# Two-term MLP up products: one 512-column matmul for two of 256, and a split evacuation

## The reference

```python
def _sq_relu_mlp(h, w_up, w_down):
    u = jax.nn.relu(h @ w_up)
    return (u * u) @ w_down
```

## Time and profile before

| | us |
|---|---|
| median of 3 runs | 1383.15 (1383.14 to 1383.69) |
| span of the profiled execution | 1382.5 |
| TensorE busy | 1346.9 (97%) |
| VectorE busy | 864.3 (63%) |
| ScalarE busy | 673.8 (49%) |
| mean granted TensorE clock | 0.991 |

### The profile page before, as it was taken

One profiled execution on the slowest core, in us unless ns is written; L12 is line 12 of the kernel. 1 busy time (PEld: TensorE's weight loads), 2 busy tenths in 40 slices (PEclk: granted clock), 3 DMA queues, 4 the chain that ended last, 5 costly groups with the idle time before them and its releaser, 6 DMA issues.

```text
span 1382.5 us, 26707 instructions
## 1 busy us (share of the span) xinstructions
PE 1346.9 (97%) x11635; PEld 1195.1 (86%) x11635; DVE 864.3 (63%) x1388; ACT 673.8 (49%) x1202; POOL 87.7 (6%) x104
## 2 busy tenths in 40 slices
PE   8999999999999999999999999999999998999997
PEld 6888998988867889998799999799987896799996
DVE  6786655573395655556685666856467556856565
ACT  6775544552384545442651224445443468545452
POOL 3000400000060000000000430000000000000000
PEclk9999999999999999999999999999999999999999
DMA  9345555453302555554233000655545451555550
GB/s 350 124 182 198 183 183 183 183 198 123 147 38 68 193 189 188 196 191 151 105 140 123 4 5 34 240 200 184 183 183 183 153 183 62 179 193 190 199 184 31
DMA packets 17635, 215.18 MB, mean 156 GB/s; under 512 B 1976, under 2 KB 2144, under 8 KB 4848
## 3 DMA queue, kind: packets, MB, share of 16 engines
q1 hardware_dynamic: 15888, 205.54, 40.3%
q0 software_dynamic: 1632, 7.94, 1.6%
HBM read 212.41 MB, written 1.06 MB: 154 GB/s over the span
## 4 chain that ended last, share of the span: by engine, by line
PE 84%; DVE 9%; ACT 4%; DMA 1%; issue 1%; SPq 0%; DVEq 0%; ACTq 0%
PE psum L665 24%; PE psum L471 11%; PE psum L472 11%; PE psum L473 11%; PE psum L1008 3%; DVE w_low L1862 3%; PE psum L1089 2%; PE psum L569 1%; PE psum L1141 1%; ACT w_high L1342 1%; PE psum L540 1%; PE psum L565 1%; PE psum L541 1%; PE psum L542 1%; DMA ring<-weights 1%; PE psum L561 1%
## 5 line engine op out<-in xcount | busy, mean ns | idle before, releaser
L1862 DVE TENSOR_TENSOR w_low<-ring,w_high 128x1024 fp32r<-128x1024 f32 x368 | 437.0, 1222 | 231.7 <-ACT w_high L1342 231.7
L1342 ACT ACTIVATE w_high<-ring 128x1024 fp32r<-128x1024 f32 x368 | 368.6, 1047 | 175.9 <-PE psum L665 155.4
L471 PE MATMUL psum<-act_split,w_high 128*128 128x256 f32 x1312 | 381.7, 291 | 3.7 <-DVE w_low L1862 3.6
L472 PE MATMUL psum<-act_split,w_high 128*128 128x256 f32 x1312 | 372.5, 284 | 0.0
L473 PE MATMUL psum<-act_split,w_low 128*128 128x256 f32 x1312 | 372.3, 284 | 0.0
L665 PE MATMUL psum<-w_high,up_split 128*128 128x512 f32 x1024 | 287.6, 391 | 0.8 <-DVE up_split L2010 0.8
L471 PEld LDWEIGHTS psum<-act_split,w_high 128*128 128x128 f32 x1312 | 252.6, 193 | 11.6 <-DVE w_low L1862 4.7
L472 PEld LDWEIGHTS psum<-act_split,w_high 128*128 128x128 f32 x1312 | 253.0, 193 | 2.6 <-issue 1.4
L473 PEld LDWEIGHTS psum<-act_split,w_low 128*128 128x128 f32 x1312 | 252.9, 193 | 0.0
L665 PEld LDWEIGHTS psum<-w_high,up_split 128*128 128x128 f32 x1024 | 190.4, 188 | 40.5 <-issue 2.7
L665 PE MATMUL psum<-w_low,up_split 128*128 128x512 f32 x512 | 163.1, 390 | 0.0
(11 more groups left out here) (338 smaller groups left out, 1661.3 us busy)
## 6 DMA issues: line engine op xcount, KB each, us to landing
ring<-weights SPq DMA_DIRECT2D x95, 2048.0 KB, 7.8
work<-rows POOLq DMA_DIRECT2D x4, 1024.0 KB, 5.0
ring<-weights SPq DMA_DIRECT2D x4, 512.0 KB, 8.5
work<-rows POOLq DMA_DIRECT2D x4, 512.0 KB, 5.6
x<-x_in SPq DMA_DIRECT2D x2, 512.0 KB, 4.4
work<-t_bias POOLq DMA_DIRECT2D x1, 1024.0 KB, 8.9
out<-x SPq DMA_DIRECT2D x4, 256.0 KB, 2.0
con<-consts SPq DMA_DIRECT2D x1, 687.0 KB, 21.6
```

What stands on the lines that cost most here:

```text
L471: mm(out, w_hi, x_hi, start=start, stop=False)
L472: mm(out, w_hi, x_lo, start=False, stop=False)
L1342: A(high[:, HIGH_SLOT[name], f], ring[:, n % RING, f], ACT.Copy).then_inc(weights_high, 1)
L1862: V.tensor_tensor(low[:, n % RING, f], ring[:, n % RING, f], high[:, HIGH_SLOT[name], f].bitcast(f32), ALU.subtract).then_inc(weights_spli ...
```

## The change

In blocks 1 to 7 the high weights meet high and low activations in one matmul of 512 columns, which leaves high x high in the first and high x low in the second half of the bank; low x high is added to the first half by a matmul of 256 columns. The two halves have to be added, and the ReLU comes after that. ScalarE copies the second half into `up_sum` (the former `up_relu`). VectorE waits for it (`up_cross`), adds the first half from PSUM, which also gives the bank back, waits with `settle()` for its own result, and computes max(sum, 0) * sum in one instruction.

```diff
--- before.py
+++ after.py
@@ -240,7 +240,7 @@
         scales = work[:, 16, :].rearrange("p (r d) -> p r d", r=2)
 
         up_split = over("up_split", 6, [P, 4, 2, T])
-        up_relu = work[:, 7, 0:1024].rearrange("p (m t) -> p m t", m=4)
+        up_sum = work[:, 7, 0:1024].rearrange("p (m t) -> p m t", m=4)
         up_sq = work[:, 7, 1024:2048].rearrange("p (m t) -> p m t", m=4)
         up_relu_tokens = work[:, 7, 0:1024].rearrange("p (h f) -> p h f", h=2)
         up_sq_tokens = work[:, 7, 1024:2048].rearrange("p (h f) -> p h f", h=2)
@@ -652,8 +652,10 @@
                             if m == 0 and k % 2 == 0:
                                 quarter_in(name, k // 2)
                             at = k * 512 + m * P
-                            last = product(bank(q, T), w_hi[:, at:at + P], w_lo[:, at:at + P],
-                                           act_split[:, k, 0, :], act_split[:, k, 1, :], k == 0, k == NC - 1)
+                            mm(bank(q), w_hi[:, at:at + P], act_split[:, k, :, :].rearrange("p s t -> p (s t)"),
+                               start=(k == 0), stop=False, skip_group_check=True)
+                            last = mm(bank(q, T), w_lo[:, at:at + P], act_split[:, k, 0, :], start=False,
+                                      stop=(k == NC - 1), skip_group_check=True)
                         last.then_inc(bank_filled, 1)
 
                     name = f"down{layer}_{b}"
@@ -1435,7 +1437,7 @@
                         split(f"down{layer}_{b}", [m])
                         q = TURN[("up", layer, b)] + m
                         filled(q)
-                        taken(A(up_relu[:, m, :], bank(q, T), ACT.Relu), q)
+                        A(up_sum[:, m, :], bank(q)[:, T:2 * T], ACT.Copy).then_inc(sig("up_cross"), 1)
                         act.wait_ge(sig("up_squared"), 4 * (FBLOCKS - 1) * layer + 4 * (b - 1) + m + 1)
                         A(up_split[:, m, 0, :], up_sq[:, m, :], ACT.Copy).then_inc(sig("up_high"), 1)
                     if b < FBLOCKS - 1:
@@ -2003,9 +2005,11 @@
                         split(f"down{layer}_{b}", [m])
                         q = TURN[("up", layer, b)] + m
                         at = 4 * (FBLOCKS - 1) * layer + 4 * (b - 1) + m + 1
-                        read_out(dve, q)
-                        V.tensor_tensor(up_sq[:, m, :], up_relu[:, m, :], up_relu[:, m, :],
-                                        ALU.mult).then_inc(sig("up_squared"), 1)
+                        dve.wait_ge(sig("up_cross"), at)
+                        taken(V.tensor_tensor(up_sum[:, m, :], bank(q, T), up_sum[:, m, :], ALU.add), q)
+                        settle()
+                        V.scalar_tensor_tensor(up_sq[:, m, :], up_sum[:, m, :], 0.0, up_sum[:, m, :],
+                                               ALU.max, ALU.mult).then_inc(sig("up_squared"), 1)
                         dve.wait_ge(sig("up_high"), at)
                         V.tensor_tensor(up_split[:, m, 1, :], up_sq[:, m, :], up_split[:, m, 0, :].bitcast(f32),
                                         ALU.subtract).then_inc(sig("up_split"), 1)
```

## The result

| | before | after |
|---|---|---|
| median of 4 runs, us | 1383.42 | 1390.12 (1388.39 to 1390.71) |
| ratio | | 1.0047 [1.0034, 1.0061] |
| span of the profiled execution, us | 1382.5 | 1388.9 |
| mean granted TensorE clock | 0.991 | 0.989 |

The kernel became 0.5% slower; the forecast was 1383.9, no measurable difference, and the range ended at 1387.3.

The account below looks back on a forecast made before the run. TensorE, busy 97% of the span, was taken as the bound, with block 7 waiting on evacuation. 1382.5 - 9.6 + 7.0 + 2 x 1.7 gave a span of 1383.3 us, a median of 1383.9; range 1380.3 to 1387.3.

Parts of the forecast that it names:

- The period of the blocks: Blocks 1 to 6 of four layers: TensorE is the bound, 0.40 us less a block, 9.6 us in all.
- The cover for the longer evacuation: Blocks 1 to 6: m-tile 3 ready 1.7 us later stays hidden, with 1.4 us of cover left.
- The price of the pair: Up product, blocks 1 to 7: 512 plus 256 columns take 347.2 ns where three 256-column matmuls took 359.7.
- The bound of 0 to 12.5: Up product: limits in ns on what a pair saves against three 256-column matmuls; 12.5 was taken.
- The evacuation: Block 7: 0.46 us more per m-tile, ready 1.74 us later, 7.0 us in four layers; TensorE stop about 2.2 us.
- The clock: After block 7's four stops: the granted TensorE clock falls, 1.7 us each, two falls likeliest.
- one to three: Number of block 7's four stops followed by a clock fall; 1382.2 to 1385.6 us, chance 0.60.
- The sum: Profiled span: 1382.5 - 9.6 + 7.0, plus 2 x 1.7, is 1383.3 us; median of runs 1383.9.
- The pair saves nothing: Rival: blocks 1 to 6 gain 0 and block 7 loses 7.4 us, giving 1390.5 us; chance 0.06.
- The rival with a saving of 2.5 ns: Up product: a pair saves only the skill page's fixed part, 1.9 us in 24 blocks, giving 1388.5 us.
- The clock falls after every one: Rival: a clock fall after all four block 7 stops, 4 x 1.7 us, giving 1387.3 us; chance 0.12.
- The clock never falls: Rival: no clock fall after block 7's stops, only -9.6 + 7.0 left, giving 1380.5 us; chance 0.17.

Follow-up runs that it names:

- e1: The kernel before with streams of single and mixed matmul widths appended after TensorE's last product; a 512/256 pair took 346.7 ns, total time not compared.
- e9: The kernel before with appended streams of 512/256 pairs entered from different widths; 353 ns a pair behind 512 columns, 346.8 behind 384; total time not compared.
- e4: The kernel before with the new pairs of 512 and 256 columns but the old evacuation; 1382.06 us against 1383.74, ratio 0.9979.
- e6: The kernel before with appended streams of pairs using the up product's own weights, activations and banks, and variants; 352.8 ns a pair as it is.
- e3: The changed kernel with the old widths, three 256-column matmuls per k-chunk, keeping the new evacuation; 1394.19 us, ratio 1.0077 against the kernel before.
- e5: The changed kernel with each m-tile's eight 512-column matmuls ahead of its eight 256-column ones; 1384.29 us, ratio 1.0011 against the kernel before.
- e7: The changed kernel with eight matmuls of zeros where TensorE stops in block 7 of each layer; 1386.82 us, ratio 1.0028 against the kernel before.

## Why the prediction was wrong

- **The period of the blocks.** Right that blocks 1 to 6 are bound by PE and that a saving there reaches the end: six periods brought six times 0.19 us. The cover for the longer evacuation held; no wait of the up product for low weights appeared.
- **The price of the pair: the step that failed.** "I take 12.5, because the down stretch changes its weights at every matmul as the new one does, and both slots are read from unbroken streams." The pair took 353 ns, not 347.2, and the down product took 0.03 us more a block: 24 x 0.19 = 4.5 us in place of 9.6. The bound of 0 to 12.5 held it; the upper end was taken. The reason was not good enough: adding the slots of two unbroken streams assumes that a stream of both runs at the sum. e1 shows that it can (346.7), e9 that behind 512 columns, which is what stands ahead in this kernel, it runs at 353; e4 shows the 353 without the new evacuation, e6 without anything beside.
- **The evacuation.** Right in its size: copy 0.39, the dependent operation 0.45 us behind the add, multiply 425 ns (424 taken), a turn of 3.46 us, a stop of 2.2. The last layer, whose stop left the clock alone, shows it bare: +1.78 us where 1.74 was worked out. e3 shows that the stop comes with the evacuation: 8.2 us of it in the four layers without the pairs, 8.7 with them.
- **The clock.** The price of a fall was right (1.64 against 1.7), the number not: three falls, two forecast, inside "one to three". Over the changed kernel, e3 and e5 the clock fell behind 8 of 12 stops of 2.0 to 2.3 us, not always in the same layers. So I read the count as a chance for each stop of that length, which one execution of each kernel can't prove; at two in three the likeliest count is three, 1.6 us more than I added. The prediction's own rows, three falls behind four stops, said so already, and it counted two.
- **The sum.** -4.5 + 7.0 + 4.9 = +7.4, against +6.4 in the span and +6.7 in the medians. Of the miss of 6.2 us, 5.1 is the pair and 1.5 the clock, less 0.4 that the stretches around gave back, where the clock of one execution differs from that of another.
- **The rivals.** "The pair saves nothing" came out nearest in time (1390.5) by luck. It saves half, and the 1390.5 left out the two falls that the forecast counted; with them it would have been 1393.9, and e3, where the pair is absent and the clock fell three times, took 1394.19. The rival with a saving of 2.5 ns left them out too, 1388.5 where 1391.9 would have stood. The Trainium skill (TensorE: Matmul & The Clock Gate, Back-to-back issue gap) has those 2.5 ns as the fixed part of an isolated matmul, and by them, as an estimate, a pair would save 2.5 ns. The traces show 6.6 ns in the kernel and 13.0 in e1 (359.7 - 346.7), so the measurements decide against it. "The clock falls after every one" was one fall away. "The clock never falls" failed: eight falls stand behind stops of 2.0 to 2.3 us. The Trainium skill (TensorE: Matmul & The Clock Gate, Why this matters for your kernels) warns only of gaps longer than these, and the measurements decide against that too.
- **The range** was too narrow because it took in the clock's cases but not the other bound of the pair, though the text had named that bound: half the saving with two or three falls is about 1389 to 1391.

## What to carry to other kernels

Price a mixture of matmul widths by a stream of that mixture, entered from the work that stands ahead of it, not by the sum of the slots of pure streams; and try the widths in groups. Where a change lengthens an evacuation, look for the one place where the consumer walks the tiles at once: here four blocks of 28 took twice what the others gave, and leaving the old form in those four turned a loss into a gain. An upper bound that stands in the sum because its reasons sound good belongs in the range with its lower bound too.

## What the runs showed of the hardware

- The same alternating stream of 512- and 256-column matmuls runs at 346.7 or at about 353 ns a pair, steadily over 32 pairs, by whether 384 or 512 (or 256) columns ran ahead of it (e1, e6, e9); pairs behind pairs keep the rate of those ahead.
- Matmuls with a weight change each: 226.7, 173.5 and 119.9 ns at 512, 384 and 256 columns, and 111 at 128 (e1): 128 columns save 9 ns against 256.
- The first 512-column matmuls behind narrow ones take longer than 0.227 us: in the changed kernel the first nine of a down product, 0.232 in the mean; in the kernel before the first four. A group of eight wide ones between narrow ones pays 0.230 each (e5, 1.84 us).
- A stop of TensorE of 2.0 to 2.3 us between dense work let the clock fall in 8 of 12 cases (changed kernel, e3, e5), at 1.6 us each; filled with matmuls of zeros it did so in none of 4 (e7).
